# Gate and up tiles of the feed-forwards as three products of 256 columns, with x moved from a place 64 bytes further on

## The chip, the cores and the metric

The kernel runs on one core of a Trainium2 chip. The metric is device time in microseconds from one launch, and shorter is better. TensorE (PE) multiplies, VectorE (DVE), ScalarE (ACT) and GpSimd (POOL) work elementwise, and the queue of SyncE (SP) starts the loads of all large weights.

## What is computed

A stack of model blocks on 256 tokens of width 1024, in float32: two layers, each with two SwiGLU feed-forwards around a mixer (a recurrent time mix, then a differential attention), and a third layer with two attentions side by side and a feed-forward whose 16384 experts are chosen by top-k of key scores. Four times, for the two layers and their two feed-forwards each, this is added to x:

```
def swiglu(h, w_in, w_out):
    gate, up = jnp.split(h @ w_in, 2, axis=-1)
    return (jax.nn.silu(gate) * up) @ w_out

x = x + 0.5 * swiglu(rms_norm(x, ffn_norm[l, 0]), ffn_w_in[l, 0], ffn_w_out[l, 0])
```

with `w_in` of 1024 x 5632 and `w_out` of 2816 x 1024. The expert layer multiplies the normed x by all 16384 rows of `peer_u`, weighs the results, and multiplies by all of `peer_v`.

## The kernel before, in words

All weights pass through PE as tiles of 128 partitions x 1024 float32 (512 KB, `TILE`). A tile is loaded into one of four raw slots; ACT copies it rounded to the matmul format fp32r (`tile_high`, L193), DVE subtracts that from the original (`tile_low`, L205; some tiles on POOL, L217), into one of three slots each. x is split in the same manner into a high and a low part. A product of the two is then made of three matmuls, high x high, high x low and low x high, summed in PSUM.

x, normed and turned so that features lie on the partitions, is one tensor `hT` of 128 x 8 x 2 x 256: eight chunks (`KC`) of 128 features, for each the high part and beside it the low part, 256 tokens each (`T`). `k.h_both` is the whole of it, `k.hT` the pair of its high and low views (L3236, L3237).

There are two ways to use it:
- Features out: x moves and the tile is the stationary operand. `feature_major` (L294) takes one tile and makes 8 x 3 products of 256 columns, by `products` (L275 to L278), into 128 output features x 256 tokens. It serves w_r and w_k (time mix), in_qk_b, peer_q and peer_u. For w_k the moving operand is `rwkv_mixed`, for peer_q `peer_first`; the others move `hT`.
- Tokens out: the tile moves in 512 columns, and 128 tokens of x or of the hidden layer are stationary. It serves the down tiles, w_kv, the gates, peer_v and others; by `products` too.

The gate and up tiles of the feed-forwards have a form of their own, `feature_major_side_by_side` (L311): high moves together with low in 512 columns against `tile_high` (L320), and high alone in 256 columns against `tile_low` (L319, and L323 for the first chunk). The bank of 512 columns then holds high x high plus low x high in its left half and high x low in its right half. ACT copies the right half out (L638 gate, L642 up), and DVE adds the left half to it (L667, L675).

A feed-forward is 22 rounds (`FC`) of a gate, an up and a down tile, the down tile one round late and the last three down tiles together at the end (`tensor_ffn`). After the additions DVE multiplies the gate by the norm's root (L671), ACT takes Silu (L647), DVE multiplies by up (L679), ACT and DVE split the hidden tile (L652, L683), and the down tile's twelve products of 512 columns add into four banks. The gate and up sums turn through four other banks; before a bank is used again, PE waits for the signal given with `bank(...)`: `gate_summed` for a gate bank, `up_summed` for an up bank. The order on each engine is written out by hand: between the steps of a round, `split_high` and `split_low` work the next three tiles.

SBUF tensors are laid out in the order of `program`: x, hT, raw_tiles, tile_high, tile_low, cols (704 bytes), ident (512), small (1024), unread (1024), minus_half (64), and then the rooms of the stages, which share one place (`rooms`). `LINE` is 16 float32, 64 bytes.

## Time and profile before

| | us |
|---|---|
| median of 3 runs | 2168.83 (2163.69 to 2174.69) |
| the profiled execution | 2168.9 |
| its span, first to last instruction | 2167.6 |
| PE, matmuls | 2107.9 busy (97%) |
| PE, weight loads | 1848.7 (85%) |
| DVE | 1532.7 (71%) |
| ACT | 1104.4 (51%) |
| POOL | 184.6 (9%) |

The mean granted clock of TensorE was 0.985 of full speed. 352 MB moved by DMA, 163 GB/s over the span. Every length of a matmul in the profile is its latency, from its first read to its modelled end; the next one starts long before that, so what a matmul costs is the distance between starts, which the timeline shows to 0.01 us. A row with a count over 1 merges neighbours and gives the length from the first start to the last end.

### The profile page before, as it was taken

To read this page: it belongs to the slowest core of one execution; us is meant where nothing else is said; L and a number is where in the kernel's file an instruction comes from. 1 tells how busy PE (TensorE), PEld (TensorE's weight loads), DVE (VectorE), ACT (ScalarE), POOL (GpSimd) and SP (SyncE) were. 2 spreads that over 40 slices of the span, in tenths; PEclk is the share of its full clock that TensorE was granted. 3 is DMA by queue.
4 is the path that set the end of the run, shared out by engine and by line. 5 is a ranking of instruction groups with operands and counts; after the bars stand their busy time and mean duration, and the time that the engine had idled before them with its cause. 6 is when DMAs were issued, how large, how long until landed. Compare 5 with 4: busy or idle time off the path is not lost.

```text
span 2167.6 us, 34080 instructions
## 1 busy us (share of the span) xinstructions
PE 2107.9 (97%) x13430; PEld 1848.7 (85%) x13430; DVE 1532.7 (71%) x2626; ACT 1104.4 (51%) x1765; POOL 184.6 (9%) x102
## 2 busy tenths in 40 slices
PE   7999999999999999889999899999999999999999
PEld 6888689888888888578889678999999999888887
DVE  5667785776676667766675676899889985555555
ACT  5554633365555555555554875544544444444443
POOL 0000003300020000110003003243000000000000
PEclk9999999999999999899999899999999999999999
DMA  6666221266655666146656235555544445565654
GB/s 198 192 188 203 88 88 60 88 182 188 193 175 178 193 188 185 59 128 192 188 183 210 93 98 195 167 164 186 166 147 147 143 142 190 192 194 193 193 193 155
DMA packets 97630, 352.47 MB, mean 163 GB/s; under 512 B 10896, under 2 KB 12688, under 8 KB 97088
## 3 DMA queue, kind: packets, MB, share of 16 engines
q1 hardware_dynamic: 97472, 350.29, 50.9%
q8 instruction: 108, 1.77, 0.3%
q14 instruction: 50, 0.41, 0.1%
HBM read 349.20 MB, written 1.05 MB: 162 GB/s over the span
## 4 chain that ended last, share of the span: by engine, by line
PE 88%; DVE 7%; ACT 3%; issue 1%; POOL 1%; DMA 0%; SPq 0%; ACTq 0%; DVEq 0%
PE psum L276 19%; PE psum L278 18%; PE psum L277 18%; PE psum L320 15%; PE psum L319 6%; PE psum L2745 2%; DVE tile_low L205 1%; PE psum L885 1%; PE psum L323 1%; ACT tile_high L193 1%; PE psum L363 1%; POOL small L1701 1%; PE psum L1083 1%; PE psum L963 1%; DVE peer_active L2952 0%
## 5 line engine op out<-in xcount | busy, mean ns | idle before, releaser
L205 DVE TENSOR_TENSOR tile_low<-raw_tiles,tile_high 128x1024 fp32r<-128x1024 f32 x598 | 740.3, 1240 | 370.1 <-ACT tile_high L193 364.5
L193 ACT ACTIVATE tile_high<-raw_tiles 128x1024 fp32r<-128x1024 f32 x642 | 677.6, 1057 | 414.0 <-PE psum L278 411.0
L320 PE MATMUL psum<-hT,tile_high 128*128 128x512 f32 x1408 | 495.8, 397 | 5.0 <-issue 5.0
L319 PE MATMUL psum<-hT,tile_low 128*128 128x256 f32 x1232 | 344.3, 279 | 0.0
L276 PE MATMUL psum<-hT,tile_high 128*128 128x256 f32 x1152 | 334.4, 290 | 2.4 <-DVE tile_low L205 2.4
L277 PE MATMUL psum<-hT,tile_high 128*128 128x256 f32 x1152 | 327.7, 284 | 0.0
L278 PE MATMUL psum<-hT,tile_low 128*128 128x256 f32 x1152 | 327.3, 284 | 0.0
L276 PE MATMUL psum<-tile_high,hT 128*128 128x512 f32 (+1 forms) x816 | 323.5, 396 | 3.5 <-DVE hT L2094 1.8
L277 PE MATMUL psum<-tile_low,hT 128*128 128x512 f32 (+1 forms) x816 | 319.8, 392 | 0.0
L278 PE MATMUL psum<-tile_high,hT 128*128 128x512 f32 (+1 forms) x816 | 319.8, 392 | 0.0
L320 PEld LDWEIGHTS psum<-hT,tile_high 128*128 128x128 f32 x1408 | 258.2, 188 | 55.8 <-issue 5.4
L319 PEld LDWEIGHTS psum<-hT,tile_low 128*128 128x128 f32 x1232 | 232.8, 189 | 8.2
L276 PEld LDWEIGHTS psum<-hT,tile_high 128*128 128x128 f32 x1152 | 222.6, 193 | 3.3 <-DVE tile_low L205 2.6
L277 PEld LDWEIGHTS psum<-hT,tile_high 128*128 128x128 f32 x1152 | 222.9, 193 | 0.0
L278 PEld LDWEIGHTS psum<-hT,tile_low 128*128 128x128 f32 x1152 | 222.7, 193 | 0.0
L276 PEld LDWEIGHTS psum<-tile_high,hT 128*128 128x128 f32 x816 | 155.7, 191 | 41.2 <-issue 5.9
L278 PEld LDWEIGHTS psum<-tile_high,hT 128*128 128x128 f32 x816 | 155.5, 191 | 32.4
L277 PEld LDWEIGHTS psum<-tile_low,hT 128*128 128x128 f32 x816 | 155.7, 191 | 31.1
L217 POOL TENSOR_TENSOR tile_low<-raw_tiles,tile_high 128x1024 fp32r<-128x1024 f32 x44 | 107.2, 2437 | 851.8 <-ACT tile_high L193 851.6
L276 PE MATMUL psum<-tile_high,ffn_hidden_high 128*128 128x512 f32 x352 | 137.3, 390 | 0.0
L278 PE MATMUL psum<-tile_high,ffn_hidden_low 128*128 128x512 f32 x352 | 136.9, 389 | 0.0
L277 PE MATMUL psum<-tile_low,ffn_hidden_high 128*128 128x512 f32 x352 | 136.9, 389 | 0.0
(367 smaller groups left out, 2661.9 us busy)
## 6 DMA issues: line engine op xcount, KB each, us to landing
raw_tiles<-ffn_in_dram SPq DMA_DIRECT2D x176, 512.0 KB, 3.9
raw_tiles<-peer_u_dram SPq DMA_DIRECT2D x128, 512.0 KB, 3.3
raw_tiles<-peer_v_dram SPq DMA_DIRECT2D x128, 512.0 KB, 4.3
raw_tiles<-ffn_out_dram SPq DMA_DIRECT2D x88, 512.0 KB, 3.6
raw_tiles<-w_kv_dram SPq DMA_DIRECT2D x16, 512.0 KB, 3.4
raw_tiles<-in_gates_dram SPq DMA_DIRECT2D x16, 512.0 KB, 3.3
raw_tiles<-peer_q_dram SPq DMA_DIRECT2D x16, 512.0 KB, 3.7
raw_tiles<-w_k_dram SPq DMA_DIRECT2D x8, 512.0 KB, 3.6
```

The source lines that it names most:

```text
L193: scalar.activation(k.high[:, n % SLOTS, :], k.raw[:, n % RAW_SLOTS, :], ACT.Copy).then_inc(*k.tile_high_made.mark(n))
L205: vector.tensor_tensor(k.low[:, n % SLOTS, :], k.raw[:, n % RAW_SLOTS, :], k.high[:, n % SLOTS, :].bitcast(F32), ALU.subtract).then_inc(*k ...
L217: pool.tensor_tensor(k.low[:, n % SLOTS, :], k.raw[:, n % RAW_SLOTS, :], k.high[:, n % SLOTS, :].bitcast(F32), ALU.subtract).then_inc(*k.p ...
L276: k.tensor.matmul(out, still[0], moving[0], start=first, stop=False)
L277: k.tensor.matmul(out, still[0], moving[1], start=False, stop=False)
L278: return k.tensor.matmul(out, still[1], moving[0], start=False, stop=last)
L319: k.tensor.matmul(ps[:, 0:T], low[:, c, :], both[:, c, 0, :], start=False, stop=False, skip_group_check=True)
L320: ins = k.tensor.matmul(ps, high[:, c, :], both[:, c, :, :], start=(c == 0), stop=(c == KC - 1), skip_group_check=True)
L323: k.tensor.matmul(ps[:, 0:T], low[:, c, :], both[:, c, 0, :], start=False, stop=False, skip_group_check=True)
L363: ins = k.tensor.transpose(ps[:, c * P:(c + 1) * P], src[:, c * P:(c + 1) * P], k.ident)
L885: ins = tensor.matmul(ps[tb][:, cols], still, tile[:, c, cols], start=False, stop=last, skip_group_check=True)
L2745: ins = tensor.matmul(ps[:, n, :], r["i_hot"](q)[:, :, n], r["j_gates"](q)[:, n // 2, w, :, n % 2], start=(w == 0), stop=(w == PARTS - 1))
```

## The change

- Each gate and up tile goes through `feature_major` into the left half of its bank, with the moving operand `k.hT_beside`: the same shape as `k.hT`, 64 bytes (a `LINE`) further on in a tensor that has grown by 64 bytes. The norm's output of the feed-forwards is written to that view.
- ACT's two copies a round and DVE's two additions go. DVE multiplies the gate bank by the root straight away, and the up bank by Silu's result. The up bank is released by `hidden_made`.
- w_r and peer_u move `k.hT_beside` too, and what makes their x writes there. in_qk_b keeps `k.hT`, as do all stages where x is stationary.
- `minus_half` (64 bytes) moves from behind `unread` to a place between hT and raw_tiles. So the tiles lie 128 bytes further on than before and all rooms 64; the rooms of the feed-forwards begin with a new unused tensor `line` of 64 bytes, and lie 128 bytes further on.

```
-def feature_major_side_by_side(k, ps, both, ready=None):
...
-        feature_major_side_by_side(k, bank(k, (s, f, "gate"), k.gate_summed, (s, f)), k.h_both, ready if f == 0 else None)
-        feature_major_side_by_side(k, bank(k, (s, f, "up"), k.up_summed, (s, f)), k.h_both)
+        feature_major(k, bank(k, (s, f, "gate"), k.gate_summed, (s, f))[:, 0:T], k.hT_beside, ready if f == 0 else None)
+        feature_major(k, bank(k, (s, f, "up"), k.hidden_made, (s, f))[:, 0:T], k.hT_beside)
...
-    scalar_x(k, s, base + SLOTS)
+    scalar_x(k, s, base + SLOTS, k.hT_beside)
...
-        if f >= 3:
-            scalar.wait_ge(*k.hidden_low_made.at((s, f - 3)))
-        scalar.wait_ge(*k.tile_used.at(gate_tile))
-        scalar.activation(r["act"][:, f % 3, 1, :], result(k, (s, f, "gate"))[:, T:2 * T], ACT.Copy).then_inc(
-            *k.low_sum_out.mark((s, f, "gate")))
         split_high(k, up + SLOTS)
-        scalar.wait_ge(*k.tile_used.at(up))
-        scalar.activation(r["act"][:, f % 3, 0, :], result(k, (s, f, "up"))[:, T:2 * T], ACT.Copy).then_inc(
-            *k.low_sum_out.mark((s, f, "up")))
...
-        vector.wait_ge(*k.low_sum_out.at((s, f, "gate")))
-        vector.tensor_tensor(r["act"][:, n, 1, :], gate[:, 0:T], r["act"][:, n, 1, :], ALU.add).then_inc(
-            *k.gate_summed.mark((s, f, "raw")))
-        vector.wait_ge(*k.gate_summed.at((s, f, "raw")))
         vector.wait_ge(*k.low_sum_out.at((s, "root")))
-        vector.tensor_tensor(r["act"][:, n, 1, :], r["act"][:, n, 1, :], r["root"][:, :], ALU.mult).then_inc(
+        vector.wait_ge(*k.tile_used.at(up - 1))
+        vector.tensor_tensor(r["act"][:, n, 1, :], gate[:, 0:T], r["root"][:, :], ALU.mult).then_inc(
             *k.gate_summed.mark((s, f)))
         split_low(k, up + SLOTS)
-        vector.wait_ge(*k.low_sum_out.at((s, f, "up")))
-        vector.tensor_tensor(r["act"][:, n, 0, :], up_sum[:, 0:T], r["act"][:, n, 0, :], ALU.add).then_inc(
-            *k.up_summed.mark((s, f)))
-        vector.wait_ge(*k.up_summed.at((s, f)))
+        vector.wait_ge(*k.tile_used.at(up))
         vector.wait_ge(*k.silu_made.at((s, f)))
-        vector.tensor_tensor(r["act"][:, n, 0, :], r["act"][:, n, 1, :], r["act"][:, n, 0, :], ALU.mult).then_inc(
+        vector.tensor_tensor(r["act"][:, n, 0, :], up_sum[:, 0:T], r["act"][:, n, 1, :], ALU.mult).then_inc(
             *k.hidden_made.mark((s, f)))
...
-        feature_major(k, ps[:, 0:T], k.hT, mix_ready(0) if g == 0 else None)
-        feature_major(k, ps[:, T:2 * T], k.hT)
+        feature_major(k, ps[:, 0:T], k.hT_beside, mix_ready(0) if g == 0 else None)
+        feature_major(k, ps[:, T:2 * T], k.hT_beside)
...
-            feature_major(k, ps[:, i * T:(i + 1) * T], k.hT, normed if (g, i) == (0, 0) else None,
+            feature_major(k, ps[:, i * T:(i + 1) * T], k.hT_beside, normed if (g, i) == (0, 0) else None,
...
-    k.h_both = sb("hT", [P, KC, 2, T], F32R)
+    room_of_h = sb("hT", [P, 2 * KC * T + LINE], F32R)
+    k.h_both, beside = (room_of_h[:, at:at + 2 * KC * T].rearrange("p (c n t) -> p c n t", n=2, t=T) for at in (0, LINE))
     k.hT = (k.h_both[:, :, 0, :], k.h_both[:, :, 1, :])
+    k.hT_beside = (beside[:, :, 0, :], beside[:, :, 1, :])
+    k.minus_half = sb("minus_half", [P, LINE])[:, :]
...
-    k.minus_half = sb("minus_half", [P, 16])[:, :]
```

## Rows read from the trace of the kernel before

**Rows 1.** The page: busy time by engine, and the chain that ended last.

```profile
PE 2107.9 (97%) x13430; PEld 1848.7 (85%) x13430; DVE 1532.7 (71%) x2626; ACT 1104.4 (51%) x1765; POOL 184.6 (9%) x102
...
PE 88%; DVE 7%; ACT 3%; issue 1%; POOL 1%; DMA 0%; SPq 0%; ACTq 0%; DVEq 0%
PE psum L276 19%; PE psum L278 18%; PE psum L277 18%; PE psum L320 15%; PE psum L319 6%; PE psum L2745 2%; DVE tile_low L205 1%; PE psum L885 1%; PE psum L323 1%; ACT tile_high L193 1%; PE psum L363 1%; POOL small L1701 1%; PE psum L1083 1%; PE psum L963 1%; DVE peer_active L2952 0%
```

**Rows 2.** Waits of PE (total, times, longest), second feed-forward, then 1440 to 1860.

```profile
PE psum L550 <- DVE ffn_diagonal L543: 0.2, 1, 0.2
...
PE psum L276 <- DVE tile_low L205: 2.4, 1, 2.4
PE psum L276 <- DVE hT L3078: 0.3, 1, 0.3
```

**Rows 3.** Groups of PE by shape: count, busy us, mean ns, idle before.

```profile
L320 PE MATMUL psum<-hT,tile_high 128*128 128x512 f32 x1408 | 495.8, 397 | 5.0 <-issue 5.0
L319 PE MATMUL psum<-hT,tile_low 128*128 128x256 f32 x1232 | 344.3, 279 | 0.0
...
L277 PE MATMUL psum<-hT,tile_high 128*128 128x256 f32 x1152 | 327.7, 284 | 0.0
...
L276 PE MATMUL psum<-peer_first_high,tile_high 128*128 128x256 f32 x128 | 36.8, 288 | 0.0
...
L276 PE MATMUL psum<-rwkv_mixed_high,tile_high 128*128 128x256 f32 x64 | 18.2, 284 | 1.4 <-DVE rwkv_mixed_low L1189 1.4
```

**Rows 4.** Timeline of PE, one round: start, length, instruction (moving, stationary), count.

```profile
63.73 0.39 PE L320 MATMUL psum<-hT,tile_high 128*128 128x512 f32 x1
63.96 0.28 PE L323 MATMUL psum<-hT,tile_low 128*128 128x256 f32 x1
64.07 0.28 PE L319 MATMUL psum<-hT,tile_low 128*128 128x256 f32 x1
64.19 0.40 PE L320 MATMUL psum<-hT,tile_high 128*128 128x512 f32 x1
...
64.78 0.28 PE L319 MATMUL psum<-hT,tile_low 128*128 128x256 f32 x1
64.90 0.40 PE L320 MATMUL psum<-hT,tile_high 128*128 128x512 f32 x1
65.14 0.28 PE L319 MATMUL psum<-hT,tile_low 128*128 128x256 f32 x1
65.25 0.40 PE L320 MATMUL psum<-hT,tile_high 128*128 128x512 f32 x1
...
66.31 0.63 PE L320 MATMUL psum<-hT,tile_high 128*128 128x512 f32 x2
66.78 0.28 PE L323 MATMUL psum<-hT,tile_low 128*128 128x256 f32 x1
...
69.32 0.39 PE L276 MATMUL psum<-tile_high,ffn_hidden_high 128*128 128x512 f32 x1
69.55 0.39 PE L277 MATMUL psum<-tile_low,ffn_hidden_high 128*128 128x512 f32 x1
...
72.05 0.39 PE L320 MATMUL psum<-hT,tile_high 128*128 128x512 f32 x1
```

**Rows 5.** Busy time by engine in the four feed-forwards.

```profile
core 0: us, PE busy (x) PEld busy (x) DVE busy (x) ACT busy (x) POOL busy (x), PEclk, DMA share, GB/s
14.70:191.10 176.40, 176.39 (x934) 151.48 (x935) 121.58 (x176) 92.77 (x150) 0.00 (x0) 1.00 0.63 190
434.20:609.80 175.60, 175.37 (x936) 150.36 (x935) 123.25 (x184) 96.07 (x159) 1.11 (x2) 1.00 0.63 188
669.00:844.00 175.00, 175.00 (x936) 150.29 (x935) 122.69 (x181) 93.33 (x153) 0.00 (x0) 1.00 0.62 187
953.30:1128.90 175.60, 175.38 (x936) 150.35 (x935) 123.23 (x184) 96.26 (x159) 1.11 (x2) 1.00 0.62 188
```

**Rows 6.** Timeline of PE in peer_u.

```profile
1500.10 0.28 PE L277 MATMUL psum<-hT,tile_high 128*128 128x256 f32 x1
1500.22 0.28 PE L278 MATMUL psum<-hT,tile_low 128*128 128x256 f32 x1
1500.34 0.28 PE L276 MATMUL psum<-hT,tile_high 128*128 128x256 f32 x1
1500.46 0.28 PE L277 MATMUL psum<-hT,tile_high 128*128 128x256 f32 x1
```

**Rows 7.** Timeline of PE: products of 16 columns.

```profile
319.32 3.64 PE L899 MATMUL psum<-rwkv_masks,rwkv_late 128*128 128x16 f32 x32
```

**Rows 8.** Weight loads, 1500 to 1540 (peer_u), then 60 to 100 (feed-forward).

```profile
L276 PEld LDWEIGHTS psum<-hT,tile_high 128*128 128x128 f32 x112 | 21.5, 192 | 0.0
...
L320 PEld LDWEIGHTS psum<-hT,tile_high 128*128 128x128 f32 x76 | 13.9, 188 | 2.8
```

**Rows 9.** Busy time of DVE in peer_u, by 40 us.

```profile
1700.00:1740.00 40.00, 37.77 (x71) 1.00 0.44 145
1740.00:1780.00 40.00, 38.89 (x72) 1.00 0.43 146
sum 240.00, DVE 219.47; mean DVE 36.58
```

**Rows 10.** Groups of DVE, then ACT, in the first feed-forward, 60 to 140.

```profile
L675 DVE TENSOR_TENSOR ffn_act<-psum,ffn_act 128x256 f32<-128x256 f32 x10 | 4.2, 424 | 5.3 <-ACT ffn_act L642 5.3
...
L667 DVE TENSOR_TENSOR ffn_act<-psum,ffn_act 128x256 f32<-128x256 f32 x9 | 3.8, 425 | 8.2 <-ACT ffn_act L638 8.2
...
L642 ACT ACTIVATE ffn_act<-psum 128x256 f32<-128x256 f32 x10 | 3.9, 387 | 13.7 <-PE psum L320 13.7
L638 ACT ACTIVATE ffn_act<-psum 128x256 f32<-128x256 f32 x9 | 3.5, 386 | 15.7 <-PE psum L320 15.7
```

More of the change, by code:

```diff
@@ L308, in feature_major @@
     return n
-def feature_major_side_by_side(k, ps, both, ready=None):
-    n, (high, low) = take(k)
-    high, low = (t.rearrange("p (k n) -> p k n", k=KC) for t in (high, low))
-    for c in range(KC):
-        if ready:
-            ready(c)
-        if c:
-            k.tensor.matmul(ps[:, 0:T], low[:, c, :], both[:, c, 0, :], start=False, stop=False, skip_group_check=True)
-        ins = k.tensor.matmul(ps, high[:, c, :], both[:, c, :, :], start=(c == 0), stop=(c == KC - 1),
-                              skip_group_check=True)
-        if c == 0:
-            k.tensor.matmul(ps[:, 0:T], low[:, c, :], both[:, c, 0, :], start=False, stop=False, skip_group_check=True)
-    ins.then_inc(*k.tile_used.mark(n))
 def tensor_features(k, stage, src, ready=None, fill=0):
@@ L658, in vector_ffn @@
     vector, r, base = k.vector, k.room[s], FIRST[s][0]
-    vector_x(k, s, base + SLOTS)
+    vector_x(k, s, base + SLOTS, k.hT_beside)
     vector.memset(r["ones"][:, :], 1.0)
@@ L1185, in mix_low @@
     def mix_low(n, half):
-        to = (r["mixed"], k.hT)[n == 0]
+        to = (r["mixed"], k.hT_beside)[n == 0]
         chunks = slice(4 * half, 4 * half + 4)
@@ L1476, in mix_high @@
     def mix_high(n, half):
-        to = (r["mixed"], k.hT)[n == 0]
+        to = (r["mixed"], k.hT_beside)[n == 0]
         chunks = slice(4 * half, 4 * half + 4)
@@ L2803, in normed_high @@
         scalar.wait_ge(*k.gain_applied.at(("peer", half)))
-        scalar.activation(k.hT[0][:, chunks, :], r["whole"][:, chunks, :], ACT.Copy).then_inc(
+        scalar.activation(k.hT_beside[0][:, chunks, :], r["whole"][:, chunks, :], ACT.Copy).then_inc(
             *k.h_high_made.mark(("peer", "normed", half)))
@@ L2909, in normed_low @@
         vector.wait_ge(*k.h_high_made.at(("peer", "normed", half)))
-        vector.tensor_tensor(four_chunks(half, k.hT[1]), four_chunks(half, r["whole"]),
-                             four_chunks(half, k.hT[0]).bitcast(F32), ALU.subtract).then_inc(
+        vector.tensor_tensor(four_chunks(half, k.hT_beside[1]), four_chunks(half, r["whole"]),
+                             four_chunks(half, k.hT_beside[0]).bitcast(F32), ALU.subtract).then_inc(
                                  *k.h_low_made.mark(("peer", "normed", half)))
@@ L3193, in room @@
         return stack
-    ffn = dict(ones=([P, P], F32), diagonal=([P, T], F32), root=([P, T], F32), act=([P, 3, 2, T], F32), hidden_high=([P, 3, T], F32R), hidden_low=([P, 3, T], F32R))
+    ffn = dict(line=([P, LINE], F32), ones=([P, P], F32), diagonal=([P, T], F32), root=([P, T], F32), act=([P, 3, 2, T], F32), hidden_high=([P, 3, T], F32R), hidden_low=([P, 3, T], F32R))
     room("ffn00", **ffn).close()
@@ L3268, in program @@
     k.low_sum_out = signal("low_sum_out")
-    k.up_summed = signal("up_summed")
     k.hidden_made = signal("hidden_made")
```

## The prediction

> **What bounds the kernel now.** I read the page first: PE is busy 97% of the span and the chain that ended last lies on PE for 88% of it; the five lines that carry it are the products of `products` (L276 to L278) and of the side-by-side helper (L319, L320) [rows 1]. The waits of PE come next: in the second feed-forward it waited 0.2 us in all, and between 1440 and 1860 us for 2.7 us [rows 2]. So what happens on ACT, DVE or the DMA queues is paid only where it makes PE wait, and nearly nothing does; the time is the number of matmuls times the distance from one start to the next. That distance isn't in the grouped lines, whose mean is the latency of one matmul (397 ns for 512 columns) while the next has long begun [rows 3]. It has to be read from the timeline: the start column.
>
> In a feed-forward one round is a gate tile, an up tile and a down tile. The gate tile starts at 63.73, the down tile at 69.32, the next gate tile at 72.05 [rows 4]. So gate and up together cost 5.59 us for 16 chunks, 0.349 us for a pair of 512 and 256 columns; the down tile costs 2.73 us for 12 products, 0.227 each. The four phases last 175 to 176.4 us each, PE is busy 175 to 176.4 of them, at full clock (PEclk 1.00), with DMA at 0.62 to 0.63 [rows 5].
>
> The three-product form can be seen in the kernel already. In the peer_u stage it moves 256 columns of x three times a chunk, and its starts are 1500.10, 1500.22, 1500.34, 1500.46: 0.120 us each, without variation [rows 6].
>
> **Part 1: gate and up tiles as three products.** A round of gate and up becomes 48 products of 256 columns instead of 16 of 512 and 16 of 256. There are 88 rounds (176 tiles; 1408 products at L320 [rows 3]). The break-even is 5.59 / 48 = 0.1165 us. At the 0.120 of [rows 6] the round costs 5.76 us, 0.17 more, in all +15 us. The number of columns streamed is the same (768 a chunk); what changes is that there are three weight loads in place of two, and each instruction adds its own fixed part. So part 1 by itself loses, and the change stands or falls with part 2.
>
> **Part 2: x 64 bytes further on.** What does a 256-column product cost at another distance between moving data and weights? The trace has no such product: by the sizes of the tensors ahead of them all of x, the tiles and the rooms begin at multiples of 128 bytes (afterwards the tiles still do, as minus_half's 64 bytes now stand ahead of them beside x's 64). So this cost is bounded, not read.
> - Upper end: 0.120, the flat value of [rows 6], if the address is of no account.
> - Lower end: 0.109. The products of L899 move 16 columns only, so nothing but the load of their 128 weight columns can set their pace: 32 of them take 3.64 us, less 0.26 for the last one's own length, over 31 steps is 0.109 [rows 7]. A full load of four-byte weights can't be followed faster than that.
> - Nearest row: the 256-column product in the gate tile that comes first, with a load beside it. From 63.96 to 64.07 is 0.11, and from 65.14 to 65.25 is 0.11, while 64.78 to 64.90 is 0.12, from the same instruction on the same kind of operands [rows 4]. So 0.11 is reached beside a weight load, and 0.12 is something added to it.
> - That something can be seen on both sides of the pair. In the peer_u stretch the loads last 192 ns, in the feed-forward stretch 188 [rows 8], and the matmuls of 256 columns last 284 ns in the three-product form against 279 at L319 [rows 3]. Both the stream and the load beside it are stretched by some 4 ns at once, as two readers that meet would be. The two tiles of a round, which have the same work and differ in where their weights lie, differ too: the row of 66.31 holds two starts, the second 0.63 - 0.40 = 0.23 later, so the gate tile takes 66.54 - 63.73 = 2.81 and the up tile 69.32 - 66.54 = 2.78 [rows 4].
> Two streams that begin together at equal distances can meet at each step of the way, and a shift of one of them by a small amount ends that. I take 0.113: the 0.11 rows with a little for the parts that the two decimals hide.
>
> A rule of the Trainium skill speaks against this. "TensorE: Matmul & The Clock Gate", in "Step-by-step: what each phase is for", says that TensorE reads the moving operand and the weights through two independent ports, and that loading the next weights takes no bandwidth from the running matmul. By it the address doesn't matter and the sum is the +15 us of part 1 alone (the first rival). The trace agrees only in part: loads do overlap, but 192 against 188 ns is no independence. The same page's section "Wait — 56ns, not 53.3ns?" gives N / 2.4 GHz plus 2.5 ns, 109 ns for 256 columns; by that estimate the sum would be near that of the lower end.
>
> The shift reaches more than the gate and up tiles. x moves in 256 columns also in peer_u (1024 chunks) and w_r (64), which are switched to the shifted view. The rooms begin 64 bytes further on because x's tensor has grown by a line, so the moving operands of w_k (64 chunks, rwkv_mixed) and peer_q (128 chunks, peer_first) are shifted as well [rows 3]. Only in_qk_b (64) keeps the old view. That is 3072 products in peer_u and 768 in the others. The feed-forward rooms get a line of padding, so that the hidden tiles stand to the weights as before: the down tiles stay at 2.73. The wide products with tile_high moving and x as weights keep their view and cost.
>
> **The sum at 0.113.**
> - Gate and up: 48 x 0.113 = 5.42 against 5.59, 0.17 less, x 88 = -15.0 us.
> - peer_u: 3072 x 0.007 = -21.5 us. DVE is near its end there: it is busy 37.77 of 40 us and then 38.89 of 40 [rows 9]. PE would shrink a stretch of 40 us with some 264 such products by 1.85 us, and the last stretch has 1.1 us of slack on DVE. I give back 2 us: -19.5.
> - w_r, w_k, peer_q: 768 x 0.007 = -5.4 us.
> - Sum -39.9 us. The profiled execution took 2168.9 us with a span of 2167.6, and the median of the runs shown is 2168.8, so both bases give 2129.
>
> **What lies beside it and costs nothing.** ACT loses two copies of a low sum a round (L638, L642: 386 and 387 ns), DVE two additions (L667, L675: 425 and 424 ns) [rows 10]; neither is late for PE, so nothing is gained but room. DVE now waits for the gate tile's last product itself, then for the up tile's. Queued behind the first wait are the splits of two tiles, which are wanted three tiles later, some 8 us; before, DVE waited there for ACT's copy of the same tile, which came later still (8.2 us idle in this stretch, ended by L638 [rows 10]). The up bank is now held until hidden_made rather than up_summed, two DVE instructions and a wait for Silu later; with four banks in turn it is wanted a whole round (8.3 us) later. If either cover were gone, a round would lose tenths of a microsecond, 88 times. The DMA queue has to deliver a round's three tiles in 8.15 instead of 8.32 us, 0.64 for 0.63 of its share.
>
> **Rivals.**
> 1. The address is of no account, the product stays at 0.120. For it: the two ports above, and the mixed_high, peer_first and x products, in different places, all stand at 0.120. Against it: those places are all alike modulo 128 bytes. It gives +15 us and nothing back, 2184, slower. Each 0.001 us is 8.1 us in the sum (4224 + 3840 products), so the change turns slower from 0.1181 on, and by half a per cent from 0.1195. Chance 0.18.
> 2. The shift takes away a part, and the product settles at 0.116 to 0.118, as the pairs of 0.117 in the feed-forward now do. At 0.116: -1.9, -11.3 and -3.1, so 2153; at 0.118: +6.5, -6.1 and -1.5, so 2168. Chance 0.12.
> 3. The meeting was all there was, and the load's own pace of 0.109 remains: 48 x 0.109 = 5.23, -31.7; peer_u -33.8 and 5 given back to DVE; others -8.4. Sum -69, 2100. Chance 0.10.
> 4. DVE becomes the bound in the whole of peer_u. It is busy 219.5 of the 240 us between 1540 and 1780 [rows 9], so PE could shrink these by at most 20 us, and wants 11. It would take away 5 us more than I gave it. It is a variant of the forecast, inside its range.
>
> **How the numbers follow.** The forecast, 0.111 to 0.115 and 2116 to 2146, gets 0.60; its time is 2129. Half a per cent is 11 us, about what a measurement of this kernel can tell from no change. Faster by more than that: the forecast, rival 3 and the lower part of rival 2, 0.74; within it 0.08; slower 0.18. The range reaches from 2108, between the forecast and rival 3, to 2185, since the cost at the upper end has 0.18 of the chance. The forecast's own range is 2116 to 2146.
>
> **What would show each step.** In the timeline of a gate tile, 24 products with starts 0.113 apart (0.120: rival 1; 0.109: rival 3), and a round of 8.15 us against 8.32. Phases of 171 to 173 us. In peer_u the same spacing, loads of 188 ns instead of 192. The down tiles at 2.73. in_qk_b, left unshifted, still at 0.120: that is the control inside the changed kernel. Waits of PE for tile_low in the end of peer_u would show the DVE part. The prediction is wrong if the spacing stays, or if the wide products, whose neighbours in the queue have moved, get another pace of their own: 3500 of them stand here at no change.

## The result, and the profile after

The changed kernel takes 2175.22 us (median of 20 runs, 2165.66 to 2182.34) against 2169.61 for the kernel before, run beside it: a ratio of 1.0025 with a 95% interval of 1.0014 to 1.0036. The forecast was 2129.0 with a range of 2108 to 2185. The time lies in the range, the forecast itself is wrong by 46 us and in its sign.

The page of the changed kernel (profiled execution 2173.89 us, span 2172.6), the lines that answer to [rows 1], and the waits of PE from 1440 to 1870 us (total, times, longest), as in [rows 2]:

```profile
PE 2109.6 (97%) x14838; PEld 1903.1 (88%) x14838; DVE 1459.8 (67%) x2450; ACT 1054.6 (49%) x1589; POOL 185.5 (9%) x102
...
PE 84%; DVE 10%; ACT 3%; issue 1%; POOL 1%; DMA 0%; SPq 0%; ACTq 0%; DVEq 0%
...
PE psum L2706 <- DVE peer_active L2960: 3.0, 2, 1.8
PE psum L276 <- DVE tile_low L205: 2.7, 1, 2.7
PE psum L276 <- DVE hT L3048: 0.4, 1, 0.4
```

PE is still the bound. It has 1408 matmuls more and stands at the same busy time; the work taken from DVE and ACT (73 and 50 us) bought nothing. In peer_u and at its end PE now waits 6.1 us for DVE, where it waited 2.7. These waits stand in the first part of the stage (1389 to 1812 us), not in its last:

```profile
1457.43 0.38 PE L276 MATMUL psum<-hT,tile_high 128*128 128x256 f32 x1 [2.66 <-DVE tile_low L205]
...
1485.03 0.30 PE L2706 MATMUL psum<-ident,peer_active 128*128 128x128 f32 x1 [1.20 <-DVE peer_active L2960]
...
1543.02 0.41 PE L2706 MATMUL psum<-ident,peer_active 128*128 128x128 f32 x2 [1.76 <-DVE peer_active L2960]
```

The timeline of one round answers to [rows 4] (start, length, instruction):

```profile
64.31 0.28 PE L276 MATMUL psum<-hT,tile_high 128*128 128x256 f32 x1
64.43 0.28 PE L277 MATMUL psum<-hT,tile_high 128*128 128x256 f32 x1
64.55 0.28 PE L278 MATMUL psum<-hT,tile_low 128*128 128x256 f32 x1
64.66 0.28 PE L276 MATMUL psum<-hT,tile_high 128*128 128x256 f32 x1
...
69.96 0.39 PE L276 MATMUL psum<-tile_high,ffn_hidden_high 128*128 128x512 f32 x1
...
72.68 0.28 PE L276 MATMUL psum<-hT,tile_high 128*128 128x256 f32 x1
```

Gate and up take 69.96 - 64.31 = 5.65 us for 48 products, 0.1177 each; 5.59 before. The down tile takes 2.72, as before (2.724 in the median of the rounds before, 2.720 now). So the shift works, 0.1177 is not 0.120, but it doesn't reach 0.113, and it lies above the break-even of 0.1165.

In peer_u ([rows 6]) two paces are found, 30 us apart in the same stage with the same operands, 0.113 and then 0.118; w_k (rwkv_mixed) runs at 0.113 to 0.114 throughout; in_qk_b, which kept its view, at 0.119 to 0.120, near the 0.120 of the forecast:

```profile
1500.13 0.28 PE L277 MATMUL psum<-hT,tile_high 128*128 128x256 f32 x1
1500.24 0.28 PE L278 MATMUL psum<-hT,tile_low 128*128 128x256 f32 x1
1500.35 0.28 PE L276 MATMUL psum<-hT,tile_high 128*128 128x256 f32 x1
...
1530.14 0.28 PE L276 MATMUL psum<-hT,tile_high 128*128 128x256 f32 x1
1530.26 0.28 PE L277 MATMUL psum<-hT,tile_high 128*128 128x256 f32 x1
1530.38 0.28 PE L278 MATMUL psum<-hT,tile_low 128*128 128x256 f32 x1
...
216.06 0.28 PE L278 MATMUL psum<-rwkv_mixed_high,tile_low 128*128 128x256 f32 x1
216.18 0.28 PE L276 MATMUL psum<-rwkv_mixed_high,tile_high 128*128 128x256 f32 x1
216.29 0.28 PE L277 MATMUL psum<-rwkv_mixed_low,tile_high 128*128 128x256 f32 x1
...
1161.76 0.28 PE L276 MATMUL psum<-hT,tile_high 128*128 128x256 f32 x1
1161.88 0.29 PE L277 MATMUL psum<-hT,tile_high 128*128 128x256 f32 x1
1162.00 0.28 PE L278 MATMUL psum<-hT,tile_low 128*128 128x256 f32 x1
```

And something that the prediction held at no change has moved: the wide products with x as weights. Busy time and count of PE in peer_v (1900 to 2100 us), before and then after:

```profile
1900.00:2100.00 200.00, 200.00 (x884) 1.00 0.60 193
...
1900.00:2100.00 200.00, 200.00 (x863) 1.00 0.59 189
```

That is 226.2 ns a product before and 231.7 after, with some two in each count that only overlap the window; the distances between starts are 226.7 and 232.4.

Where the time went, by kind of product (mean distance between starts in each trace, pauses left out; all starts, so finer than two decimals):

| products | count | before ns | after ns | difference us |
|---|---|---|---|---|
| round of a feed-forward | 88 | 8313 | 8373 | +5.3 |
| wide, x as weights, peer_v | 1535 | 226.7 | 232.4 | +8.7 |
| wide, x as weights, elsewhere | 912 | 221.7 | 225.8 | +3.7 |
| peer_u, products | 3072 | 119.9 | 116.0 | -12.0 |
| peer_u, waits of PE | | 2.7 us | 6.1 us | +3.4 |
| w_r and w_k | 384 | 119.9 | 113.5 | -2.5 |
| peer_q | 384 | 119.8 | 117.2 | -1.0 |
| in_qk_b | 192 | 119.8 | 119.0 | -0.2 |

The 912 hold 48 products of 256 columns, which bring their mean down. The sum is +5.4; the spans differ by +5.0. So close an agreement is in part luck: from its first product to the first of peer_v the peer_u stage shrank by 7.2 us (426.7 to 419.5), not by the 8.6 of its two rows, and stretches outside the table differ as well.

### The profile page after: what moved, and what is told of

It is laid out like the page before. It is cut to its first block, busy times and chain, and to the rows that moved or that the text cites. A ratio compares the mean times of both kernels' runs of the same rounds, so it can differ in the third digit from the quotient of the medians.

```text
span 2172.6 us, 36468 instructions
## 1 busy us (share of the span) xinstructions
PE 2109.6 (97%) x14838; PEld 1903.1 (88%) x14838; DVE 1459.8 (67%) x2450; ACT 1054.6 (49%) x1589; POOL 185.5 (9%) x102
## 4 chain that ended last, share of the span: by engine, by line
PE 84%; DVE 10%; ACT 3%; issue 1%; POOL 1%; DMA 0%; SPq 0%; ACTq 0%; DVEq 0%
PE psum L276 25%; PE psum L278 25%; PE psum L277 25%; DVE tile_low L205 2%; PE psum L2715 2%; PE psum L855 1%; ACT tile_high L193 1%; DVE peer_active L2922 1%; PE psum L347 1%; POOL small L1671 1%; PE psum L1053 1%; PE psum L933 1%; ACT hT L490 1%; DVE peer_active L2950 0%; DVE peer_active L2943 0%
## 5 line engine op out<-in xcount | busy, mean ns | idle before, releaser
L276 PE MATMUL psum<-hT,tile_high 128*128 128x256 f32 x2560 | 727.1, 284 | 8.0 <-DVE tile_low L205 8.0
L277 PE MATMUL psum<-hT,tile_high 128*128 128x256 f32 x2560 | 718.6, 281 | 0.0
L278 PE MATMUL psum<-hT,tile_low 128*128 128x256 f32 x2560 | 718.5, 281 | 0.0
L276 PEld LDWEIGHTS psum<-hT,tile_high 128*128 128x128 f32 x2560 | 483.2, 189 | 12.5 <-issue 5.7
L278 PEld LDWEIGHTS psum<-hT,tile_low 128*128 128x128 f32 x2560 | 489.7, 191 | 0.0
L277 PEld LDWEIGHTS psum<-hT,tile_high 128*128 128x128 f32 x2560 | 483.7, 189 | 3.1
L276 PE MATMUL psum<-tile_high,hT 128*128 128x512 f32 (+1 forms) x816 | 326.9, 401 | 3.1 <-DVE hT L2064 1.7
L278 PE MATMUL psum<-tile_high,hT 128*128 128x512 f32 (+1 forms) x816 | 323.1, 396 | 0.0
L2826 ACT ACTIVATE peer_active<-psum 128x304 f32<-128x304 f32 (+31 forms) x64 | 20.4, 318 | 125.6 <-DVE peer_active L3000 125.6
L278 PEld LDWEIGHTS psum<-tile_high,ffn_hidden_low 128*128 128x128 f32 x352 | 66.1, 188 | 13.7
L276 PEld LDWEIGHTS psum<-tile_high,ffn_hidden_high 128*128 128x128 f32 x352 | 66.1, 188 | 10.7
L277 PEld LDWEIGHTS psum<-tile_low,ffn_hidden_high 128*128 128x128 f32 x352 | 66.1, 188 | 10.7
```

The lines of the kernel that those rows point to most:

```text
L276: k.tensor.matmul(out, still[0], moving[0], start=first, stop=False)
L277: k.tensor.matmul(out, still[0], moving[1], start=False, stop=False)
L278: return k.tensor.matmul(out, still[1], moving[0], start=False, stop=last)
```

## The experiments

"Distance" below is the start of x (where it moves) less the start of the tiles, modulo 256 bytes; the starts are those of the built kernels. Before, it is 0 for everything that meets a tile. In the changed kernel x stands 192 on from the tiles where it moves in 256 columns, and 128 on where it is weights, and in in_qk_b too. Six questions, in the order in which they came up.

**1. Is it the address, and how does the pace depend on it?** A bench with the other engines at rest; it computes nothing of the reference, as do the other three benches.

```
for xo, to in THREE:        # starts of x and of the tiles, modulo 256
    marker()                # six bf16 products
    three(xo, to, 4)        # 96 products of 256 columns
    down(to, to)            # twelve of 512
    three(xo, to, 4)
```

> A kernel of its own, which computes nothing of the reference (x is copied to the output): TensorE runs blocks of products with the other engines idle. Each block of 96 three-product matmuls of 256 columns (moving x, weights from the tiles) comes once after six bf16 products and once after twelve products of 512 columns; then blocks of 60 products of 512 columns with x as weights; then the 512 plus 256 form. Between blocks only the starts of x and of the tiles change, modulo 256 bytes (x minus tiles: 0, 16, 32, 64, 96, 128, 160, 192, 224). Theory (the distance modulo 256 sets the pace): 256 columns at distance 0 give 120 ns a product, at 192 give 113 to 118, the 512-column products give 227 at 0 and 231 to 232 at 128, the same for every pair of starts with the same distance. Rival 1 (the 118 of the changed feed-forwards and peer_u is traffic of ACT, DVE and the DMAs): 113 here in every block at 192. Rival 2 (what ran before the block picks the pace): the two blocks of one distance differ, 113 and 118.

Its timeline, a row for a block of neighbours (first start to last end); distance 0, then distance 192:

```profile
30.36 11.76 PE L69 MATMUL psum<-x_moved,tiles 128*128 128x256 f32 x96
...
44.71 11.67 PE L69 MATMUL psum<-x_moved,tiles 128*128 128x256 f32 x96
...
213.68 11.14 PE L69 MATMUL psum<-x_moved,tiles 128*128 128x256 f32 x96
...
227.39 11.47 PE L69 MATMUL psum<-x_moved,tiles 128*128 128x256 f32 x96
```

Less a last product's 0.28 and over 95 steps: 120.8 and 119.9 ns at 0; 114.3 (in the block's later part 113.3) and 117.8 at 192. So the address decides, with no other engine at work, and the first rival (0.120 whatever the address) falls. With both operands moved by 128 bytes (tiles at 0 in place of 128) the first blocks stay as they are: 120.8 and 120.8 at distance 0, 118.7 and 118.7 at 64, 119.6 and 119.5 at 128, 114.3 and 114.4 at 192. The weight loads beside these products change with them; blocks after bf16 products, distance 0, then 192:

```profile
L69 PEld LDWEIGHTS psum<-x_moved,tiles 128*128 128x128 f32 x92 | 11.1, 192 | 0.0
...
L69 PEld LDWEIGHTS psum<-x_moved,tiles 128*128 128x128 f32 x94 | 10.7, 188 | 0.0
```

At 192 the pace is 113 to 114 after the bf16 products and 118 after twelve wide products. Both paces of peer_u are here. The two blocks also begin at another of the three tile slots and in another bank; in the bench of question 4 every round has the same slots and the banks turn, and there the two paces come again by what ran before. The wide products with x as weights took 226.7 ns at 0, 233.3 at 32 and 64 and 232.5 at 128 (after the twelve products of the first tile, which are slower): the 226.7 and 232.4 of the two kernels.

**2. Which part costs what?** The layout of the change alone, with the old side-by-side form and x unshifted (a distance of 128):

```
-    k.h_both = sb("hT", [P, KC, 2, T], F32R)
+    room_of_h = sb("hT", [P, 2 * KC * T + LINE], F32R)
+    k.h_both = room_of_h[:, 0:2 * KC * T].rearrange("p (c n t) -> p c n t", n=2, t=T)
+    k.minus_half = sb("minus_half", [P, LINE])[:, :]
```

> The kernel before with the memory layout of the changed one: 64 bytes behind hT, minus_half ahead of the tiles, the line in the feed-forward rooms; x is used at its old place, gate and up in the 512 plus 256 form. The tiles so lie 128 bytes further from x than before. Theory (distance of tiles and x): the 2400 products of 512 columns with x as weights go from 227 to 231-232 ns, +10 to +11 us, ratio 1.005. Rival (these products got slower in the changed kernel because of what runs beside them, not by the layout): ratio 1.000, 227 ns.

2179.34 us, ratio 1.0039 (1.0025 to 1.0052), 4 us above the whole change, though the two intervals overlap. A round takes 8353 ns, 40 more, with nothing of its code changed; peer_v has the 232.4 ns of the changed kernel:

```profile
1900.00:2100.00 200.00, 200.00 (x862) 1.00 0.57 189
```

The three-product form alone, in the old layout:

```
-    room_of_h = sb("hT", [P, 2 * KC * T + LINE], F32R)
-    ... for at in (0, LINE))
+    room_of_h = sb("hT", [P, 2 * KC * T], F32R)
+    ... for at in (0, 0))
```

> The changed kernel in the memory layout of before, x at its old place: only the three-product form and what goes with it on ACT and DVE. Theory: 120 ns a product at distance 0 in the feed-forwards too, 5.76 us a round for gate and up, 88 x 0.17 = +15 us, ratio 1.007. Rival (the feed-forward's engines shake the pace loose from 120, or fewer ACT and DVE steps give something back): 116 to 118 ns, ratio 1.000 to 1.002.

2180.73 us, 1.0049 (1.0030 to 1.0067). The down tile, the next gate tile, the next down tile:

```profile
71.06 0.40 PE L276 MATMUL psum<-tile_high,ffn_hidden_high 128*128 128x512 f32 x1
73.81 0.28 PE L276 MATMUL psum<-hT,tile_high 128*128 128x256 f32 x1
79.56 0.40 PE L276 MATMUL psum<-tile_high,ffn_hidden_high 128*128 128x512 f32 x1
```

Gate and up are 5.75 us, 0.120 a product, as part 1 of the prediction has it. The down tile takes 2.75 in place of 2.72, so a round grows by 187 ns, 16.5 us in 88 rounds; the span grows by 11.4 only. Of the rest, 3.4 lie between the third and the fourth feed-forward (113.1 us before, 109.7 here), where the granted clock differs from execution to execution (0.89 and 0.92 in these two); no product of that stretch was changed. By the distances between starts, the change is made of +16.5 for the form, -11.2 for the shift in the feed-forwards (88 rounds from 8500 to 8373 ns), -15.7 for the shift elsewhere, +12.4 for the wide products and +3.4 of waits, the +5.4 of the table.

**3. Can the wide products be put back?** `cols` (704 bytes) in place of `minus_half` (64) between hT and the tiles; x moves at a distance of 64, as weights it stands at 0:

```
-    k.minus_half = sb("minus_half", [P, LINE])[:, :]
+    k.cols = sb("cols", [P, -(-N_COLS // LINE) * LINE])[:, 0:N_COLS]
```

> The changed kernel with cols (704 bytes) between hT and the tiles and minus_half back behind unread, so that x (64 bytes further on) and the tiles lie a multiple of 256 plus 64 apart, and x as weights a multiple of 256 from them, as before; the line of the feed-forward rooms is three lines long, which keeps the hidden tiles at a multiple of 256 from the tiles. Theory: the 512-column products go back to 227 ns (-10 us against the changed kernel); products of 256 columns stay at 113 to 118 as at 192: ratio 0.998 to 0.980 to the kernel before. Rival (64 is not like 192): products of 256 columns at 120, ratio 1.007.

2169.34 us, 0.9996 (0.9981 to 1.0010). The wide products are back at 226.7 ns, worth the 12 us; the round rises to 8413 ns at this distance, 3.5 us in 88 rounds. The span is 8.6 us below that of the changed kernel, as these two make it. It is the layout that moved the wide products, and it is reversible. If so, the old form with only w_r and peer_u moved should win:

```
 (the kernel before, with cols between hT and the tiles, and)
-            feature_major(k, ps[:, i * T:(i + 1) * T], k.hT, ...
+            feature_major(k, ps[:, i * T:(i + 1) * T], k.hT_beside, ...
```

> The feed-forwards as before (512 plus 256 form, x at its old place), x 64 bytes further on in w_r and peer_u alone (and the moving operands of w_k and peer_q by their rooms), with cols between hT and the tiles, so that x as weights and the hidden tiles keep their distance from the tiles modulo 256. Theory: feed-forwards and 512-column products as before; 3840 products at 118 instead of 120, -8 us, ratio 0.996, less what DVE gives back in peer_u. Rival (the pattern of 113 is entered there): 3840 x 7 ns, -25 us, ratio 0.989. Rival (DVE takes it all back): 1.000.

2161.39 us, 0.9968 (0.9951 to 0.9985), faster than both kernels. Its round is 8313 ns, and its peer_u products 117.7; the stage is 7.4 us shorter than before.

**4. Is there a faster place?** Two benches of whole feed-forward rounds (48 products, then 12 wide), steady after the first round. First at multiples of 16 bytes, with twelve more arrangements whose low tiles lie 64, 128 or 192 bytes off the high ones; then at the other multiples of 4 bytes, with 112 at both ends:

```
for form, xo, to, lo in ROUNDS:
    marker()
    for _ in range(4):
        (three if form == "three" else side)(xo, to, 2, lo)
        down(to, to, lo)
```

> A kernel of its own again (nothing of the reference is computed, x is copied to the output; the other engines are idle): for each arrangement four whole rounds as in a feed-forward, 48 products of 256 columns and 12 of 512 (hidden as weights, at distance 0 from the tiles), after six bf16 products. First the 512 plus 256 form at x minus tiles = 0, 64, 128, 192, then the three-product form at 0, 16, 32 up to 240, then at 0, 32, 64, 192 with the low tiles 64, 128, 192 bytes off the high ones. Theory (several stable patterns; the products of 512 columns ahead of a gate tile lead into the slow one): the old form at 0 takes 8.32 us a round as in the kernel before; three products at 0 take 8.49, at 64 and 192 8.37 to 8.40 in every round, none below 8.32. Rival (once the pattern of 113 ns is reached in a round it is kept over the down tile): 8.15 to 8.2 us a round at 192 after the first.

> The round of 48 products of 256 columns and 12 of 512, three times over, other engines idle (nothing of the reference is computed): x minus tiles at 112 first and last, and between them at every multiple of 4 bytes that is no multiple of 16. In the coarser scan a round took 8.23 us at 112, 8.53 at 96 and at 128, 8.35 at 32, 8.37 at 192, 8.50 at 0. Theory (a line of 16 or more bytes is what counts): distances within 16 bytes of each other take the same time, so 100 to 108 like 96. Rival (each element's place counts, as the two readers meet by time and place): single distances differ from their neighbours by up to 0.2 us, and there are others at or below 8.25. Either way 112 gives 8.23 at both ends.

The old form takes 8.313 us at 0 and 8.353 at 128; the three-product form 8.500 at 0, 8.413 at 64, 8.373 at 192, the values of the kernels to the nanosecond, in a bench without a DMA or another engine beside it. With high and low tiles alike, one distance stands out, 112, at 8.227. One arrangement with the low tiles 128 bytes off the high ones and x 192 on was faster still, 8.213; no kernel tried it. Distances 192 and then 112 in the first of these benches:

```profile
580.22 5.71 PE L69 MATMUL psum<-x_moved,tiles 128*128 128x256 f32 x48
585.77 2.90 PE L93 MATMUL psum<-tiles,hidden 128*128 128x512 f32 x12
588.51 5.82 PE L69 MATMUL psum<-x_moved,tiles 128*128 128x256 f32 x48
...
417.30 5.64 PE L69 MATMUL psum<-x_moved,tiles 128*128 128x256 f32 x48
422.78 2.91 PE L93 MATMUL psum<-tiles,hidden 128*128 128x512 f32 x12
```

At 192 the first block, after bf16 products, takes 5.55 us, and the second, after a down tile, 5.65, with the same tile slots in both; the third and fourth take 5.65 in other banks too. In a feed-forward a gate tile comes after a down tile, so it gets the slow pattern of that place. At 112 it is 5.48. The second bench shows how narrow this is: 108, 112 and 116 bytes give 8.487, 8.227 and 8.586 us.

**5. Does it carry into the kernel?** Four kernels were to have x 112 bytes on, in the new and the old form of the feed-forward:

```
-    room_of_h = sb("hT", [P, 2 * KC * T + LINE], F32R)
+    room_of_h = sb("hT", [P, 2 * KC * T + 36], F32R)
-    ... for at in (0, LINE))
+    ... for at in (36, 0))
```

> The changed kernel with x at 112 bytes from the tiles modulo 256 where it moves in 256 columns (the tensor of x grows by 144 bytes, the aligned view lies 144 bytes into it, the shifted view at its start; the tiles follow at once; minus_half goes into the tail of cols). x as weights and the hidden tiles keep distance 0 to the tiles. The signal that frees two chunks of x in the last peer_u tile is given one chunk later. Theory (distance and entry set the pattern, and the bench's round carries over): a round of 8.23 us against 8.32 in the kernel before, -7 to -8 us in the four feed-forwards; peer_u at 113 to 114, 3072 x 6 ns = -19 us less some 5 that DVE gives back; w_r and w_k -2; in all -22 us, ratio 0.990. Rival (the other engines' accesses upset the fast pattern, which the bench doesn't have): 118, -8 us in peer_u, nothing in the feed-forwards, 0.996. Rival (DVE holds peer_u at the 420 us of the last run): -7.5 and -8, 0.993.

> The same memory layout, with the feed-forwards in the old 512 plus 256 form at distance 0; only w_r, w_k and peer_u move x at 112. Theory: the feed-forwards as in the kernel before, peer_u as in the run beside it, so slower than that by 7 to 8 us: ratio 0.9935. Rival (the form in the feed-forwards makes no difference once x is at 112 for the rest): equal to the run beside it.

2187.33 us, 1.0072 (1.0056 to 1.0088), and 2180.48, 1.0042 (1.0027 to 1.0056). Both expectations missed, since the place was missed: a tensor begins at a multiple of 32 bytes, the tiles had slid, and x moved at 96 in place of 112 (and in the old form's feed-forward, and wherever it is weights, at 240 in place of 0). At these distances the bench has 8.527 and, as question 6 showed, 8.420 us; the kernels' rounds are 8527 and 8420 ns.

With the tiles inside hT's tensor the distance is a true 112, the tiles beginning at 16 modulo 256:

```
+    at_tiles = 2 * KC * T + 36
-    k.high = sb("tile_high", [P, SLOTS, TILE], F32R)
+    k.high, k.low = (room_of_h[:, a:a + SLOTS * TILE]... for a in (at_tiles, at_tiles + SLOTS * TILE))
```

> As the run at 112 before, but with the places mended: SBUF tensors begin at multiples of 32 bytes, so there the tiles stood 96 bytes from x and not 112. Here the high and low tiles are part of x's own tensor, 112 bytes (modulo 256) from where x moves and 0 from where x is the weights; the hidden tiles lie 16 bytes into their tensor, at 0 from the tiles; rwkv_mixed is at 112. Theory (the distance sets the round to the nanosecond, as 8.313, 8.353, 8.373, 8.413, 8.500 and 8.527 us of the six kernels against 8.313, 8.353, 8.373, 8.413, 8.500 and 8.526 of the bench at their distances): a round of 8.227 us, 88 x 0.086 = -7.6 us in the feed-forwards; peer_u at 114 to 118 with DVE near its end, -8 to -19 us; w_r and w_k -1 to -2; ratio 0.987 to 0.992. Rival (112 is only good with idle engines): a round of 8.37 or more, ratio above 0.997.

> The same places, feed-forwards in the old 512 plus 256 form with x at distance 0 (round of 8.313 us), w_r and peer_u at 112. Theory: as the run beside it but 7.6 us slower, ratio 0.9905 to 0.9955. Rival (DVE or the bf16 products of the lots bring peer_u back to 118 or more): no better than with x 64 bytes on, 0.997.

2200.95 us, 1.0137 (1.0113 to 1.0160), and 2181.94, 1.0052 (1.0032 to 1.0072). Here my theory fell: the distance was right, and the round was 8533 ns:

```profile
71.63 0.39 PE L276 MATMUL psum<-hT,ffn_hidden 128*128 128x512 f32 x1
74.41 0.28 PE L276 MATMUL psum<-hT 128*128 128x256 f32 x1
80.17 0.39 PE L276 MATMUL psum<-hT,ffn_hidden 128*128 128x512 f32 x1
```

5.76 us for gate and up, 0.120 a product, at the distance that gave 0.114 in the bench. The rounds make 88 x 0.220 = 19.4 of the 32 us by which the span grew. Some 10 more are in peer_v: at a distance of 0 its wide products took 233.3 ns here and 230.0 in the old-form kernel, at the same addresses, where every kernel with tiles at 128 and that distance has 226.7. Either the tiles' own place counts beside the distance, or the kernel disturbs the pattern.

**6. The distance alone, or the tiles' own place too?** A bench over four starts of the tiles, and a kernel in each form with the tiles at a start that the bench had used (128 modulo 256) and x 112 on, in w_r and peer_u and, in the new form, in the feed-forwards:

```
-    room_of_h = sb("hT", [P, 2 * KC * T + LINE], F32R)
+    room_of_h = sb("hT", [P, 2 * KC * T + 28], F32R)
-    k.minus_half = sb("minus_half", [P, LINE])[:, :]
+    k.cols = sb("cols", [P, 10 * LINE])[:, :]      # the last five columns go to a small tensor behind
```

> A bench of TensorE alone, which computes nothing of the reference: three rounds of a feed-forward in the changed form for tiles starting at 128, 144, 160 and 176 modulo 256, each with x 0, 16, ... 240 bytes beyond; then the old form for the same tile places at eight distances. Theory A (the distance alone counts): the rows of the four tile places are equal, 8.227 us at a distance of 112 in each. Theory B (the tile's own place counts too): tiles at 144, 160 and 176 (not multiples of 64) pay some 4 to 9 ns in each of the 12 hidden products, and their rows differ from those at 128; then the bench gives what the kernels showed: 8.527 us for tiles at 160 with x 96 on, 8.533 us for tiles at 144 with x 112 on, 8.307 us for the old form with tiles at 144 and x 112 on, 8.420 us for the old form with tiles at 160 and x 96 on.

> The changed kernel with its SBUF laid out so that the tiles and the wide copies stand at 128 modulo 256 and x, where it moves in 256 columns of the feed-forwards, of w_r, w_k, peer_q and peer_u, 112 bytes beyond the tiles (the mixed and first-half copies of the RWKV stage at 64). Nothing of the computation is left out. Theory (each pair of places has its pace, and the bench shows it): a feed-forward round takes 8.227 us, 86 ns less than before, so 88 rounds give 7.6 us; wide and hidden products stay at 227 ns; peer_u at 114 to 118 ns a product gives 8 to 19 us: ratio 0.987 to 0.993. Rival (the fast pattern needs the bench's quiet surroundings or its entry): a round of 8.37 us or more, ratio 0.997 or more.

> The same layout with the feed-forward of before (side-by-side products of 512 and 256 columns). Nothing of the computation is left out. Theory: a round stays near the 8.313 us of before, the rest gains as in the run beside it, so this kernel is about 7.6 us slower than that one: ratio 0.990 to 0.9965. Rival (the fast pattern does not carry over): both kernels within 2 us of each other or this one the faster.

The bench, steady round in us (second gate tile to third), three-product form, by distance:

```
distance    0    16    32    64    96   112   128   144   192   240
at 128  8.500 8.460 8.347 8.414 8.527 8.226 8.520 8.320 8.373 8.354
at 160  8.500 8.460 8.346 8.414 8.527 8.226 8.520 8.320 8.373 8.354
at 144  8.458 8.432 8.449 8.474 8.560 8.533 8.527 8.527 8.200 8.446
at 176  8.458 8.402 8.459 8.213 8.560 8.533 8.527 8.518 8.200 8.445
```

Distance 112 with the tiles at 128, then with the tiles at 144:

```profile
219.89 5.64 PE L69 MATMUL psum<-x_moved,tiles 128*128 128x256 f32 x48
225.37 2.91 PE L93 MATMUL psum<-tiles,hidden 128*128 128x512 f32 x12
...
635.23 5.92 PE L69 MATMUL psum<-x_moved,tiles 128*128 128x256 f32 x48
640.99 2.94 PE L93 MATMUL psum<-tiles,hidden 128*128 128x512 f32 x12
```

The tiles' own place counts, but not as I had put it: 128 and 160 are alike at every distance, and 16 bytes further on the table is another one. 144 and 176 are within 0.03 us of each other at the distances shown except 64, so 32 bytes are not without effect there (and some of their rounds still change by up to 0.05 from one to the next). All four numbers of the kernels of question 5 are in the bench: 8.527, 8.533, 8.307 (old form, tiles at 144; its feed-forward x is at 0) and 8.420 (old form, tiles at 160, x at 240), so nothing in those kernels disturbed the pattern; they stood in slow places. Their tiles are at 32 and 16 modulo 256, 128 bytes from the 160 and 144 of the bench; that 128 bytes on both operands change nothing was measured in question 1, with tiles at 0 and 128 only, and these four agreements bear it out.

The three-product kernel takes 2150.76 us (2145.23 to 2153.64), ratio 0.9905 (0.9882 to 0.9928); the old form in the same layout 2159.18, 0.9953 (0.9933 to 0.9972). A round of the first, and its waits for DVE in peer_u and at its end (total, times, longest):

```profile
69.95 0.39 PE L278 MATMUL psum<-tile_high,ffn_hidden_high 128*128 128x512 f32 x1
72.69 0.28 PE L278 MATMUL psum<-hT,tile_high 128*128 128x256 f32 x1
78.17 0.39 PE L278 MATMUL psum<-tile_high,ffn_hidden_high 128*128 128x512 f32 x1
...
PE psum L278 <- DVE tile_low L207: 5.6, 1, 5.6
PE psum L2708 <- DVE peer_active L2962: 3.3, 2, 2.3
PE psum L278 <- DVE hT L3050: 0.4, 1, 0.4
```

Its round is 8227 ns, as in the bench; the other's 8313. The two kernels are 8.4 us apart in the median and 7.3 in the profiled spans; the forecast was 88 x 0.086 = 7.6. So the change as it was meant, three products and x further on, does win 19 us, in another place. Its peer_u products take 114.6 ns, but PE waits 9.3 us in and after that stage against 2.7 before, so the 16.3 us saved on the products (3072 x 5.3 ns) are 6.1 on the stage (426.7 to 420.6). 6.6 of the difference are these waits; the other 3.6 I did not follow. DVE is the bound at three spots in the first part of the stage (1443, 1471 and 1529 us), not in the whole of it as the fourth rival has it. In w_k and peer_q, whose operands stand in the rooms, x is 64 on from the tiles in both kernels and not 112.

## Why the prediction was wrong

**What bounds the kernel, and part 1.** Right. PE is at 97% before and after. The three-product form at 0.120 costs 5.75 us for gate and up, against 5.76 worked out; the 0.02 that the down tile after it loses (2.75 for 2.72, 88 times) was not in the sum.

**Part 2, that the shift matters.** Right in kind. The product goes from 0.120 to less wherever x moved, and in_qk_b stayed near it (119.0 ns). It was a weaker control than the prediction took it for: its view stayed, but its distance to the tiles went from 0 to 128, where the bench has 118.7 to 120.0. Loads of 188 ns in place of 192, which the prediction named as a sign, are in the bench at 192. That the load and the moving operand meet, as the prediction has it, fits these loads and the equal pace when both operands move together; it is not shown, since no run took the load away. The Trainium skill's "TensorE: Matmul & The Clock Gate", in "Step-by-step: what each phase is for", has loads that take no bandwidth from the running matmul. Question 1 speaks against that, at 120.8 against 114.3 ns for the same instructions at two distances.

**The step that failed: the term 0.113.** I had taken it from two single distances of 0.11 in [rows 4]. They are the low end of a swing: over the first feed-forward of the kernel before, the 305 distances from a product of L319 to the next wide one are 117.3 ns in the mean, from 112 to 120, and [rows 4] by itself gives 0.349 - 0.227 = 0.122 for the 256-column product of a pair. The other thing that I did not see is that a place has more than one pattern, and that the one it runs in hangs on what came before. In the changed kernel 0.113 is real in w_r, in w_k and in a part of peer_u, and in the feed-forwards it is 0.1177. Gate and up: -15.0 forecast, +5.3 measured, a miss of 20. peer_u: -21.5 forecast for the products, -12.0 measured, a miss of 9.5. w_r, w_k and peer_q: -5.4 forecast, -3.5 measured; of these only peer_q missed. By its price it was the second rival, 0.116 to 0.118, at 0.12 of the chance.

**The step that was not priced: "the wide products keep their view and cost".** They kept their view, but the tiles moved 128 bytes on, and I had counted only the distances that the diff names. It cost 12.4 us. The last sentence of the prediction had named it as what would make it wrong; it needed a term and bounds in the sum. With the terms at their measured sizes the sum is 2168.9 + 5.3 - 12.0 + 3.4 + 12.4 - 3.7 = 2174.3, and the profiled execution took 2173.9.

**peer_u's DVE.** I gave 2 us back for it, and it was 3.4 at a product of 116 ns and 6.6 at 114.6. The place was wrong too. I had read the limit from the last stretches of [rows 9], 1700 to 1780 us; there PE waited for nothing in the changed kernel (DVE busy 76.3 of the 80 us), and all waits but the 0.4 at the end stand between 1457 and 1543. So busy time near the whole of a stretch did not say where DVE would hold PE up.

**What was held at no cost.** The down tiles' 2.72 us (2.73 in the prediction), the removed work of ACT and DVE, and the later release of the up bank came out as forecast. Between the first and the last down tile of the four phases PE never stopped, as the windows show ([rows 5] has the phases with their edges):

```profile
28.00:200.73 172.73, 172.73 (x1225) 162.49 (x1225) 101.38 (x127) 79.04 (x106) 0.00 (x0) 1.00 0.57 189
...
sum 690.87, PE 690.87 PEld 649.92 DVE 404.90 ACT 316.10 POOL 3.13; mean PE 172.72 PEld 162.48 DVE 101.23 ACT 79.03 POOL 0.78
```

## What to carry to other kernels

Where PE is the bound, the pace of a matmul is read from starts, never from a row's mean length, and a change that moves an SBUF tensor by some bytes can change the pace of every product whose operands it moves against each other: list the start of each moving and stationary operand modulo 256 before and after, for the lines that the diff does not touch too. The pace of a new placing is measured, with the whole sequence of the round and not with one product repeated; a bench on TensorE alone gave each of the kernels' rounds to a nanosecond.

## What the hardware showed unexpectedly

- The mean distance between starts of 256-column fp32r products, each with a 128-column load beside it, was 113.3 ns (tiles at 144, x 192 on) to 124.1 (tiles at 128, x 132 on) in the steady rounds of the benches, by the places of the operands alone; a 512-column product with x as weights took 226.7 to 233.3 once steady.
- One placing has several steady patterns. At a distance of 192: 113.3 ns after bf16 products, 117.8 after wide ones. Inside a kernel w_k ran at 113.3 ns in the old-form kernel of question 6 and at 117.8 in the three-product one, whose operands lie at the same addresses (a distance of 64). What picks the pattern was not settled.
- Four bytes count (8.487, 8.227, 8.586 us at 108, 112, 116), and so do 16 bytes of the tiles' place at an equal distance of 112 (8.226 against 8.533). No rule that gives the pace from the addresses was found, only the table.
- The fastest place of the bench, 8.200 us with the tiles at 144 or 176 and x 192 on, was not tried in the kernel.
